# Experts: the prompt's 32 tokens go down in plain float32, a quarter of the output channels in each column quarter of TensorE

## The chip, the cores and the metric
The kernel runs on one core of one Trainium2 chip. The metric is device time in microseconds (us), the median over runs of the whole kernel. TensorE is the matmul engine (PE in the profile, PEld its weight loads), VectorE is DVE, ScalarE is ACT, GpSimd is POOL, and SyncE (SP) issues loads. SBUF is the on-chip memory of 128 partitions, PSUM the memory into which TensorE writes, in banks of 512 float32 per partition.

## The reference, cut to what matters
One layer of a two-branch network over 2048 sample tokens and 256 prompt tokens, 1024 channels wide: a convolution and an attention branch, an output projection, then a mixture of 16 experts in which every expert chooses its tokens, 256 of the samples and 32 of the prompt, and a last norm. All in float32.

```python
def ec_moe(h, w_router, w_g, w_u, w_d):
    B, n, D = h.shape
    cap = EC_FACTOR * n // N_EXPERTS
    aff = jax.nn.softmax((h @ w_router).astype(jnp.float32), axis=-1)
    vals, idx = lax.top_k(aff.transpose(0, 2, 1), cap)
    xg = jax.vmap(lambda hb, ib: hb[ib])(h, idx)
    a = jnp.einsum('becd,edf->becf', xg, w_g)
    u = jnp.einsum('becd,edf->becf', xg, w_u)
    y = jnp.einsum('becf,efd->becd', jax.nn.silu(a) * u, w_d) * vals[..., None].astype(h.dtype)
    return jax.vmap(lambda ib, yb: jnp.zeros((n, D), yb.dtype).at[ib.reshape(-1)].add(yb.reshape(-1, D)))(idx, y)
```

`ec_moe` is called once for the sample tokens (cap 256) and once for the prompt (cap 32), with the same weights; its result is scaled by the gate g2 of the branch and added to x.

## The kernel before, in words
The program is a row of phases, each a block in which every engine has its own instruction list and semaphores order them: front (modulation, first norm, input projection, convolution taps), latents, attention, mix, output projection with the router, ranking (`topk_phase`), experts (`moe_phase`), last norm. Phases don't overlap.

Precision: a product of float32 operands is built from three float32r matmuls. Each operand is split into hi (a rounded copy) and lo (the rest), and hi x hi, hi x lo and lo x hi are added in PSUM. Two places use plain float32 matmuls, which leave two records each in the trace: the values of attention (line 1177), in two column halves of the array, and the rows of the modulation in the front phase (line 388), whose outputs lie at partitions 0, 32, 64 and 96.

`topk_phase` writes `tab` [128, 16 experts, 3, 2]: for each expert three columns of up to 128 tokens (two for the samples, one for the prompt, 32 rows of it used), each with the token's row number and its router value. The prompt's part is ranked first, on 16 partitions, turned by two small transposes (lines 2000 and 2001) and copied into `tab` at the end (lines 1988 and 1989).

`moe_phase` handles an expert in M = 4 pieces of 128 hidden channels; piece q = 4e + m. The first two and the last two experts are written out, the twelve between run in a loop of six turns with two experts each. The engines work as follows, each list in its own order:
- SyncE (lines 2080 to 2090) loads for each piece `raw_gu` (1 MB of gate and up weights) and `raw_d` (512 KB of down weights), two slots of each. A load of `raw_gu` waits until GpSimd has split the piece two back, one of `raw_d` until VectorE has.
- ScalarE makes the hi parts of the weights (lines 2151, 2172), the silu of the gate (2175), the hi part of the hidden vectors (2177) and of the turned tokens (2156).
- GpSimd makes the lo part of gate/up (2112, one instruction of 2048 elements per partition), issues the gathers of an expert's tokens (2098), the scatters of its results (2107, an indirect DMA that adds to rows of x2: 128, 128 and 32 rows of 4 KB), and in the first six pieces the look-ups of later experts' tables (2118).
- VectorE makes the lo part of the down weights (2229), the hidden vectors `hid` = up x silu(gate) (2235), their lo part (2237) and of the tokens (2204), and at m = 0 the scaled result of the expert before: `scale_y` (2212), three instructions of 1024 elements, one per token tile.
- TensorE (lines 2274 to 2310) runs in each piece 48 gate/up matmuls of 288 columns (256 sample tokens and 32 of the prompt), then, for m > 0, four transposes that turn a part of the next expert's tokens, the down matmuls of the piece before for the two sample tiles (12 of 512 columns), four more transposes, and the down matmuls of the third tile (6). In these the hidden vectors are the stationary operand, 128 tokens wide, and the weights of 512 output channels the moving one. The third tile has 32 tokens; `h_hi` and `h_lo` are padded to 128 with zeros. The results of the four pieces add up in `py`, three times two PSUM banks. At m = 1 the first down matmul overwrites `py` and waits for `y_done`, the end of `scale_y`.

In the front phase the rows of the modulation (lines 380 to 389) come behind a tile of the input projection, and ahead of them TensorE waits for its own last matmul:

```python
                    if b == NBL - 1:
                        pe.wait_ge(o_done, n + 1)
                        pe.sem_inc(tile_done, 1)
```

Of the kernel before, what the change touches and what calls it, by code (L numbers as in the profile page):

```python
# [1851 lines left out]
def topk_phase(nc, t, affT, tab, pos, ident):  # L1852
# [13 lines left out]
    with ExitStack() as ctx:  # L1866
# [5 lines left out]
        topp, atp, atpf = p.sb("topp", [E, CAPP]), p.sb("atp", [E, CAPP], U32), p.sb("atpf", [E, CAPP])  # L1872
        cand, low, kept = (p.sb(n, [P, 1], U32) for n in ("cand", "low", "kept"))
# [12 lines left out]
        tp = p.ps("tp", [CAPP, 2, E])  # L1886
# [7 lines left out]
        with nc.Block() as block:  # L1894
# [12 lines left out]
            def _(dve):  # L1907
# [27 lines left out]
                dve.tensor_scalar(atpf[:], atp[:], 1.0, float(S), ALU.mult, ALU.add).then_inc(atp_done, 1)  # L1935
                dve.wait_ge(ld, 16 * LOADS)
# [51 lines left out]
                dve.tensor_copy(tab[0:CAPP, :, 2, 0].bitcast(U32), tp[:, 0]).then_inc(out_done, 1)  # L1988
                dve.tensor_copy(tab[0:CAPP, :, 2, 1], tp[:, 1]).then_inc(out_done, 1)
# [7 lines left out]
            def _(pe):  # L1997
                pe.wait_ge(atp_done, 1)
                pe.wait_ge(max_done, CAPP // 8)
                pe.transpose(tp[:, 0], atpf[:], ident[0:E, 0:E])  # L2000
                pe.transpose(tp[:, 1], topp[:], ident[0:E, 0:E]).then_inc(tp_done, 1)
# [15 lines left out]
def moe_phase(nc, t, tab, pos, ident):  # L2017
# [6 lines left out]

    TOK = CAP + CAPP
    TOKP = 3 * P
    M = FF // P
    SL = ((0, P), (P, P), (CAP, CAPP))
    with ExitStack() as ctx:
        p = Scope(nc, ctx, "moe")  # L2030
        raw_gu, raw_d = p.sb("raw_gu", [P, 2, 2, KD, P]), p.sb("raw_d", [P, 2, D])
# [4 lines left out]
        act_g, hid = p.sb("act_g", [P, TOK]), p.sb("hid", [P, TOK])  # L2036
        h_hi, h_lo = p.sb("h_hi", [P, 2, TOKP], F32R), p.sb("h_lo", [P, 2, TOKP], F32R)
        yo = p.sb("yo", [P, 3, D])
        gate = p.sb("gate", [P, 2, D])
        idx_g, idx_s = p.sb("idx_g", [P, 2, 3], U32), p.sb("idx_s", [P, 2, 3], U32)  # L2040
        val_s = p.sb("val_s", [P, 2, 3])
        bank = [p.ps("g", [P, BLK]), p.ps("u", [P, BLK])]
        py = p.ps("py", [P, 3, D])
        gate_ld = p.sem("gate_ld")
        gu_ld, d_ld = p.sems("gu_ld", 2), p.sems("d_ld", 2)
# [6 lines left out]
        zero_done, may_issue = p.sem("zero_done"), p.sem("may_issue")  # L2052
# [21 lines left out]
        with nc.Block() as block:  # L2074
            @block.sync
            def _(sp):
                for s in range(2):
                    sp.dma_start(gate[:, s], t["mod"][s, 5 * D:6 * D].partition_broadcast(P)).then_inc(gate_ld, 16)

                def load(e, u, first, last):  # L2080
                    for m in range(M):
                        q = M * e + m
                        if not (first and m < 2):
                            sp.wait_ge(glo_done, q - 1)
                        sp.dma_start(raw_gu[:, m % 2], t["w_gate_up"][bass.ds(q, 1)].rearrange("o p g k n -> (o p) g k n")
                                     ).then_inc(gu_ld[m % 2], 16)
# [6 lines left out]
            def _(pool):  # L2093
# [7 lines left out]
                def scatter(e, u):  # L2101
# [4 lines left out]
                    for i, (_, n) in enumerate(SL):  # L2106
                        pool.indirect_dma_start(t["x2"], bass.IndirectOffsetOnAxis(ap=idx_s[0:n, u, i:i + 1], axis=0),
                                                yo[0:n, i], None, compute_op=ALU.add).then_inc(y_st[i], 16)
# [16 lines left out]
                for b in (h_hi, h_lo):  # L2125
                    pool.memset(b[:, :, TOK:].bitcast(F32), 0.0).then_inc(zero_done, 1)
# [20 lines left out]
            def _(act):  # L2147
# [16 lines left out]
                def expert(e, u, first, last):  # L2164
                    for m in range(M):
# [3 lines left out]
                        act.wait_ge(d_ld[slot], 16 * (2 * e + m // 2) + 16)  # L2169
                        if not (first and m < 2):  # L2170
                            act.wait_ge(d_mm, q - 1)
                        act.activation(d_hi[:, slot], raw_d[:, slot], ACT.Copy).then_inc(dhi_done, 1)  # L2172
# [4 lines left out]
                        act.activation(h_hi[:, slot, 0:TOK], hid[:], ACT.Copy).then_inc(hhi_done, 1)  # L2177
# [6 lines left out]
            def _(dve):  # L2184
# [7 lines left out]
                def pick_s(e, u):  # L2192
                    dve.wait_ge(gate_ld, 32)
# [13 lines left out]
                def scale_y(e, u):  # L2207
                    dve.wait_ge(d_mm, M * e + M)
                    dve.wait_ge(pick_s_done, 2 * e + 2)
                    for i, (_, n) in enumerate(SL):  # L2210
                        wait(dve, y_st[i], 16 * e)
                        dve.scalar_tensor_tensor(out=yo[0:n, i], in0=py[0:n, i], scalar=val_s[0:n, u, i:i + 1],
                                                 in1=gate[0:n, i // 2], op0=ALU.mult, op1=ALU.mult).then_inc(y_done, 1)
# [5 lines left out]
                dve.wait_ge(gate_ld, 32)  # L2219

                def expert(e, u, first, last):
                    for m in range(M):
# [6 lines left out]
                        dve.tensor_tensor(d_lo[:, slot], raw_d[:, slot], d_hi[:, slot].bitcast(F32), ALU.subtract  # L2229
# [7 lines left out]
                        dve.tensor_tensor(h_lo[:, slot, 0:TOK], hid[:], h_hi[:, slot, 0:TOK].bitcast(F32), ALU.subtract  # L2237
# [10 lines left out]
            def _(pe):  # L2248
# [7 lines left out]
                def down(q, slot, first_piece, last_piece, part):  # L2256
                    for i in part:
                        for h, w in ((h_hi, d_hi), (h_hi, d_lo), (h_lo, d_hi)):
                            for n in range(2):
                                mm = pe.matmul(py[:, i, n * BLK:(n + 1) * BLK], h[:, slot, i * P:(i + 1) * P],  # L2260
                                               w[:, slot, n * BLK:(n + 1) * BLK],
# [265 lines left out]
```

## Time and profile before

| | us |
|---|---|
| median of 3 runs | 3421.84 |
| lowest, highest | 3418.48, 3424.2 |
| the profiled execution, whole | 3415.4 |
| its span, first to last instruction | 3413.5 |
| TensorE matmuls busy | 3067.7 (90%) |
| VectorE busy | 2008.2 (59%) |
| ScalarE, GpSimd busy | 1031.9, 1008.2 |

The span and all rows below come from the one profiled execution. "Busy" is the union of an engine's instructions. Matmuls overlap in the records, so the duration of one (0.39 us for 512 columns) is longer than the spacing at which they follow each other; costs on TensorE are read from start to start. `128*128 128x512` is a matmul with 128 rows by 128 stationary columns and 512 moving ones.

### The profile page before, as it was taken

What the parts mean: (1) busy time and instruction counts of PE and PEld (TensorE: products, weight loads), DVE (VectorE), ACT (ScalarE), POOL (GpSimd) and SP (SyncE); (2) the same over time, 40 slices, a digit from 0 to 9 for tenths busy, and PEclk for the clock granted to TensorE, in tenths of its full rate; (3) what the DMA queues carried; (4) which work ended last, traced back from release to release, by engine and by line L of the source; (5) the groups of instructions that cost most, each with busy time, mean ns of one, the idle gap of its engine ahead of it and who ended that gap; (6) DMA issues with size and microseconds to landing.
All of it is one profiled execution on the core that took longest, in us unless ns stands there. A gap on an engine that the chain in (4) does not pass through costs nothing. (4 is left out here: it accounts for less than half of the span.)

```text
span 3413.5 us, 44579 instructions
## 1 busy us (share of the span) xinstructions
PE 3067.7 (90%) x17172; PEld 2510.0 (74%) x17172; DVE 2008.2 (59%) x2516; ACT 1031.9 (30%) x1401; POOL 1008.2 (30%) x652
## 2 busy tenths in 40 slices
PE   7999999997969999999999799899925999999990
PEld 7788888885756666666677577778824899999990
DVE  2518384665467777777777645444474555555643
ACT  3411111111433333333333232123302333333332
POOL 0000000000113333333333443211105755655551
PEclk8999999998979999999999999999956999999995
DMA  5312131324320111011010155554304656666656
GB/s 180 112 44 101 65 132 51 108 71 137 144 66 6 29 25 28 14 23 31 6 25 19 52 184 186 191 165 146 124 5 148 186 187 186 203 190 185 187 155 241
DMA packets 135392, 370.16 MB, mean 108 GB/s; under 512 B 19478, under 2 KB 43900, under 8 KB 124828
## 3 DMA queue, kind: packets, MB, share of 16 engines
q1 hardware_dynamic: 97596, 266.60, 23.8%
q0 software_dynamic: 22080, 73.51, 7.6%
q10 hardware_dynamic: 15552, 27.79, 2.2%
q8 instruction: 111, 1.82, 0.2%
q14 instruction: 53, 0.43, 0.0%
HBM read 264.92 MB, written 102.89 MB: 108 GB/s over the span
## 5 line engine op out<-in xcount | busy, mean ns | idle before, releaser
L1231 DVE TENSOR_REDUCE at_mpart<-at_mx 128x2 f32<-128x512 f32 x574 | 369.3, 684 | 168.7 <-PE at_mx L1165 167.4
L1078 ACT ACTIVATE at_w<-at_sc 128x1024 f32<-128x1024 f32 (+1 forms) x296 | 299.4, 1013 | 546.3 <-PE at_sc L1141 515.6
L1119 POOL TENSOR_TENSOR at_part<-at_part,at_w 128x512 f32<-128x512 f32 x224 | 299.7, 1338 | 402.8 <-ACT at_w L1078 399.6
L2112 POOL TENSOR_TENSOR moe_gu_lo<-moe_raw_gu,moe_gu_hi 128x2048 fp32r<-128x2048 f32 x64 | 297.7, 4657 | 134.5 <-ACT moe_gu_hi L2151 134.1
L493 DVE SCALAR_TENSOR_TENSOR fr_r<-fr_r,fr_dw 128x2334 f32<-128x2334 f32 x120 | 318.0, 2650 | 3.9
L368 PE MATMUL fr_po<-hT_hi,fr_w_hi 128*128 128x512 f32 (+1 forms) x800 | 296.9, 371 | 2.1 <-PE fr_tp L368 1.2
L1177 PE MATMUL at_acc<-at_w,V 128*64 128x256 f32 (+1 forms) x2368 | 297.3, 388 | 0.0
L368 PE MATMUL fr_po<-hT_lo,fr_w_hi 128*128 128x512 f32 (+1 forms) x800 | 294.6, 368 | 0.0
L368 PE MATMUL fr_po<-hT_hi,fr_w_lo 128*128 128x512 f32 (+1 forms) x800 | 294.4, 368 | 0.0
L1259 DVE TENSOR_TENSOR at_part<-at_part,at_w 128x512 f32<-128x512 f32 x224 | 262.9, 1174 | 20.0 <-ACT at_w L1078 7.7
L2229 DVE TENSOR_TENSOR moe_d_lo<-moe_raw_d,moe_d_hi 128x1024 fp32r<-128x1024 f32 x64 | 190.2, 2971 | 107.1 <-ACT moe_d_hi L2172 107.1
L1177 PEld LDWEIGHTS at_acc<-at_w,V 128*64 128x64 f32 x2368 | 156.4, 138 | 91.5 <-issue 14.2
L244 POOL DMA_DIRECT2D fr_wm<-w_ada_rows x32 | 16.9, 532 | 649.9 <-PE fr_acc L388 649.9
L368 PEld LDWEIGHTS fr_po<-hT_hi,fr_w_hi 128*128 128x128 f32 x800 | 150.7, 188 | 38.7 <-issue 13.2
L287 ACT ACTIVATE fr_r<-fr_po 128x512 f32<-128x512 f32 (+1 forms) x100 | 55.6, 556 | 390.4 <-PE fr_po L368 390.4
L368 PEld LDWEIGHTS fr_po<-hT_lo,fr_w_hi 128*128 128x128 f32 x800 | 150.7, 188 | 25.4
L368 PEld LDWEIGHTS fr_po<-hT_hi,fr_w_lo 128*128 128x128 f32 x800 | 150.8, 189 | 25.1
L2286 PE MATMUL moe_g<-moe_x_hi,moe_gu_hi 128*128 128x288 f32 x512 | 152.9, 299 | 9.3 <-POOL moe_gu_lo L2112 9.3
L2286 PE MATMUL moe_g<-moe_x_hi,moe_gu_lo 128*128 128x288 f32 x512 | 152.7, 298 | 0.0
L2286 PE MATMUL moe_g<-moe_x_lo,moe_gu_hi 128*128 128x288 f32 x512 | 152.3, 297 | 0.0
L2286 PE MATMUL moe_u<-moe_x_hi,moe_gu_hi 128*128 128x288 f32 x512 | 151.5, 296 | 0.0
L2286 PE MATMUL moe_u<-moe_x_hi,moe_gu_lo 128*128 128x288 f32 x512 | 151.0, 295 | 0.0
(336 smaller groups left out, 7096.7 us busy)
## 6 DMA issues: line engine op xcount, KB each, us to landing
moe_raw_gu<-w_gate_up SPq DMA_DIRECT2D x64, 1024.0 KB, 5.6
moe_raw_d<-w_down SPq DMA_DIRECT2D x64, 512.0 KB, 3.6
fr_wm<-w_ada_rows POOLq DMA_DIRECT2D x32, 512.0 KB, 4.6
gates_scratch<-fr_r ACTq DMA_DIRECT2D x64, 256.0 KB, 2.0
mx_gates<-gates_scratch SPq DMA_DIRECT2D x64, 256.0 KB, 2.9
fr_raw<-w_in SPq DMA_DIRECT2D x28, 512.0 KB, 4.4
fr_r<-x POOLq DMA_DIRECT2D x18, 512.0 KB, 4.5
op_m_raw<-mixed_scratch SPq DMA_DIRECT2D x9, 1024.0 KB, 5.7
```

What stands on the lines that cost most here:

```text
L244: pool.dma_start(wm[:, n % 2].rearrange("p h n -> p (h n)"), t["w_ada_rows"][n]).then_inc(wm_ld[n % 2], 16)
L287: act.activation(stage[:, n % PO, 0:size], po[:, n % PO, 0:size], ACT.Sigmoid if KINDS[j] == "g" else ACT.Copy).then_inc(out_done, 1)
L368: mm = pe.matmul(out[:, 0:size], w[:, s, k, :], h[:, k, tok:tok + size], start=first, stop=final)
L493: dve.scalar_tensor_tensor(out=conv, in0=v[:, w:w + CW], scalar=scalar, in1=conv, op0=ALU.mult, op1=ALU.add).then_inc(taps, 1)
L1078: act.activation(w[:, g % NW, :, 0:n], sc[:, 2 * (g % 2):2 * (g % 2) + 2, 0:n], ACT.Exp, scale=SM_SCALE).then_inc(exp_done, 1)
L1119: pool.tensor_tensor(part[:, j % 2, 1, 0:n], before, w[:, g % NW, 1, 0:n], ALU.add).then_inc(add_p, 1)
L1177: mm = pe.matmul(acc[half * DV:(half + 1) * DV, j % 2, 0:n], V[:, h, key_tiles(b, c) + k, :], w[:, g % NW, k, half * n:(half + 1) * n], st ...
L1231: dve.tensor_reduce(mpart[:, 2 * half:2 * half + 2, c], max_bank(m, half), AX.X, ALU.max).then_inc(red_done[half], 1)
L1259: dve.tensor_tensor(part[:, j % 2, 0, 0:n], before, w[:, g % NW, 0, 0:n], ALU.add).then_inc(add_d, 1)
L2112: pool.tensor_tensor(gu_lo[:, slot], raw_gu[:, slot], gu_hi[:, slot].bitcast(F32), ALU.subtract).then_inc(glo_done, 1)
L2229: dve.tensor_tensor(d_lo[:, slot], raw_d[:, slot], d_hi[:, slot].bitcast(F32), ALU.subtract).then_inc(dlo_done, 1)
L2286: mm = pe.matmul(bank[g][:, 0:TOK], w[:, slot, g, k], x[:, u, k], start=(k == 0 and w is gu_hi and x is x_hi), stop=(k == KD - 1 and x is ...
```

## The change
In the experts' phase the third token tile leaves the common path. Its hidden vectors are taken in plain float32, straight from `hid`, and the down weights straight from `raw_d`; four matmuls of 256 moving columns replace the six of 512. Matmul g computes output channels 256g to 256g + 255 for the 32 tokens and writes them to PSUM partitions 32g to 32g + 31 of `y3` [128, 256]. So the result of the prompt has 128 rows of a quarter of the channels. It is scaled by one VectorE instruction of 256 elements, with the router values repeated four times and a gate laid out in the same way, and scattered as 128 rows of 1 KB with indices 4 x row + g into x2 seen as rows of a quarter. `raw_d` gets four slots, `hid` two, `h_hi` and `h_lo` lose their padding, `tab` a fourth column. The ranking prepares the repeated values and the indices.

```diff
@@ topk_phase
+        quarter, four = p.sb("quarter", [E, 4, CAPP]), p.sb("four", [E, 4, CAPP])
-        tp = p.ps("tp", [CAPP, 2, E])
+        tp = p.ps("tp", [P, 3, E])
                 dve.tensor_scalar(atpf[:], atp[:], 1.0, float(S), ALU.mult, ALU.add).then_inc(atp_done, 1)
+                dve.wait_ge(max_done, CAPP // 8)
+                for g in range(4):
+                    dve.tensor_scalar(quarter[:, g], atp[:], 4.0, float(4 * S + g), ALU.mult, ALU.add).then_inc(atp_done, 1)
+                    dve.tensor_copy(four[:, g], topp[:]).then_inc(atp_done, 1)
-                dve.tensor_copy(tab[0:CAPP, :, 2, 0].bitcast(U32), tp[:, 0]).then_inc(out_done, 1)
-                dve.tensor_copy(tab[0:CAPP, :, 2, 1], tp[:, 1]).then_inc(out_done, 1)
+                dve.tensor_copy(tab[0:CAPP, :, 2, 0].bitcast(U32), tp[0:CAPP, 0]).then_inc(out_done, 1)
+                dve.tensor_copy(tab[:, :, 2, 1], tp[:, 1]).then_inc(out_done, 1)
+                dve.tensor_copy(tab[:, :, 3, 0].bitcast(U32), tp[:, 2]).then_inc(out_done, 1)
-                pe.transpose(tp[:, 0], atpf[:], ident[0:E, 0:E])
-                pe.transpose(tp[:, 1], topp[:], ident[0:E, 0:E]).then_inc(tp_done, 1)
+                pe.transpose(tp[0:CAPP, 0], atpf[:], ident[0:E, 0:E])
+                pe.transpose(tp[:, 1], four[:].rearrange("e g n -> e (g n)"), ident[0:E, 0:E])
+                pe.transpose(tp[:, 2], quarter[:].rearrange("e g n -> e (g n)"), ident[0:E, 0:E]).then_inc(tp_done, 1)
@@ moe_phase, SyncE
-                for s in range(2):
-                    sp.dma_start(gate[:, s], t["mod"][s, 5 * D:6 * D].partition_broadcast(P)).then_inc(gate_ld, 16)
+                sp.dma_start(gate[:], t["mod"][0, 5 * D:6 * D].partition_broadcast(P)).then_inc(gate_ld, 16)
+                for g in range(4):
+                    sp.dma_start(gate3[g * CAPP:(g + 1) * CAPP, :],
+                                 t["mod"][1, 5 * D + g * QD:5 * D + (g + 1) * QD].partition_broadcast(CAPP)).then_inc(gate_ld, 16)
-                        if not (first and m < 2):
-                            sp.wait_ge(dlo_done, q - 1)
-                        sp.dma_start(raw_d[:, m % 2], t["w_down"][bass.ds(q * P, P), :]).then_inc(d_ld[m % 2], 16)
+                        if not first:
+                            sp.wait_ge(d_mm, q - 3)
+                        sp.dma_start(raw_d[:, m], t["w_down"][bass.ds(q * P, P), :]).then_inc(d_ld[m], 16)
@@ GpSimd
+                    pool.indirect_dma_start(t["x2"].rearrange("t (g n) -> (t g) n", g=4),
+                                            bass.IndirectOffsetOnAxis(ap=idx_s[:, u, 3:4], axis=0),
+                                            yo3[:], None, compute_op=ALU.add).then_inc(y_st[2], 16)
-                for b in (h_hi, h_lo):
-                    pool.memset(b[:, :, TOK:].bitcast(F32), 0.0).then_inc(zero_done, 1)
@@ ScalarE
-                        act.activation(h_hi[:, slot, 0:TOK], hid[:], ACT.Copy).then_inc(hhi_done, 1)
+                        act.activation(h_hi[:, slot], hid[:, slot, 0:CAP], ACT.Copy).then_inc(hhi_done, 1)
@@ VectorE
+                    wait(dve, y_st[2], 16 * e)
+                    dve.scalar_tensor_tensor(out=yo3[:], in0=y3[:], scalar=val_s[:, u, 2:3], in1=gate3[:],
+                                             op0=ALU.mult, op1=ALU.mult).then_inc(y_done, 1)
-                        wait(dve, hhi_done, q)
-                        wait(dve, hlo_done, q)
-                        dve.tensor_tensor(hid[:], bank[1][:, 0:TOK], act_g[:], ALU.mult).then_inc(hid_done, 1)
+                        if not (first and m < 2):
+                            dve.wait_ge(hhi_done, q - 1)
+                            dve.wait_ge(hlo_done, q - 1)
+                            dve.wait_ge(d_mm, q - 1)
+                        dve.tensor_tensor(hid[:, slot], bank[1][:, 0:TOK], act_g[:], ALU.mult).then_inc(hid_done, 1)
@@ TensorE
+                def down_prompt(slot, piece):
+
+                    for g in range(4):
+                        mm = pe.matmul(y3[g * CAPP:(g + 1) * CAPP, :], hid[:, slot, CAP:TOK], raw_d[:, piece, g * QD:(g + 1) * QD],
+                                       start=(piece == 0), stop=(piece == M - 1), skip_group_check=True)
+                    mm.then_inc(d_mm, 1)
-                            down(q - 1, 1 - slot, m == 1, m == 0, (0, 1))
+                            down(1 - slot, m == 1, m == 0)
-                            down(q - 1, 1 - slot, m == 1, m == 0, (2,))
+                            down_prompt(1 - slot, (m - 1) % M)
```

## Rows read from the trace of the kernel before

**Rows 1.** Stretches: us, PE, PEld, DVE, ACT, POOL busy (below: PE alone), clock, DMA, GB/s.
```profile
2700.00:3300.00 600.00, 595.95 (x3810) 547.02 (x3809) 340.81 (x314) 228.29 (x291) 347.29 (x132) 1.00 0.61 189
...
2687.20:2690.50 3.30, 3.30 (x15) 0.50 0.68 228
```

**Rows 2.** Timeline, TensorE, a piece without transposes: start, length, what.
```profile
3024.47 0.63 PE L2260 MATMUL moe_py<-moe_d_hi,moe_h_hi 128*128 128x512 f32 x2
...
3028.60 0.29 PE L2286 MATMUL moe_g<-moe_x_hi,moe_gu_hi 128*128 128x288 f32 x1
```

**Rows 3.** Timeline, TensorE: transposes and third tile of a piece with both.
```profile
3004.65 0.60 PE L2253 MATMUL moe_u<-identity,moe_xg 128*128 128x128 f32 x4
3005.00 0.71 PE L2260 MATMUL moe_py<-moe_d_hi,moe_h_hi 128*128 128x512 f32 x2
...
3006.47 0.29 PE L2286 MATMUL moe_g<-moe_x_hi,moe_gu_hi 128*128 128x288 f32 x1
```

**Rows 4.** Timeline around line 388 (four column quarters); then its records in two short windows.
```profile
271.14 0.28 PE L368 MATMUL fr_po<-hT_hi,fr_w_lo 128*128 128x256 f32 x1
271.26 0.28 PE L368 MATMUL fr_po<-hT_lo,fr_w_hi 128*128 128x256 f32 x1
271.68 1.04 PE L388 MATMUL fr_acc<-fr_wm,silu 128*2 128x512 f32 x8
272.65 0.50 PE L368 MATMUL fr_po<-hT_hi,fr_w_hi 128*128 128x512 f32 x1
272.99 0.39 PE L368 MATMUL fr_po<-hT_hi,fr_w_lo 128*128 128x512 f32 x1
...
L388 PE MATMUL fr_acc<-fr_wm,silu x4: 589/591/591, 271.7 to 271.7; 128*2 128x512 f32 x4
...
L388 PE MATMUL fr_acc<-fr_wm,silu x4: 590/592/592, 272.1 to 272.1; 128*2 128x512 f32 x4
```

**Rows 5.** Timeline around line 1177 (two column halves); then first pair and all (ns min/median/max).
```profile
1500.95 0.28 PE L1165 MATMUL at_mx<-room 96*128 96x256 f32 x1
...
1501.16 1.95 PE L1177 MATMUL at_acc<-at_w,V 128*64 128x256 f32 x16
1503.04 0.50 PE L1139 MATMUL at_sc<-room 97*128 97x512 f32 x1
...
L1177 PE MATMUL at_acc<-at_w,V x2: 430/430/430, 1501.2 to 1501.2; 128*64 128x256 f32 x2
...
L1177 PE MATMUL at_acc<-at_w,V x2368: 272/379/690, 995.3 to 1944.9; 128*64 128x256 f32 x192, 128*64 128x128 f32 x6
```

**Rows 6.** Timeline, GpSimd and TensorE, up to the eighth piece.
```profile
2682.30 9.09 POOL L2112 TENSOR_TENSOR moe_gu_lo<-moe_raw_gu,moe_gu_hi 128x2048 fp32r<-128x2048 f32 x2
...
2686.94 0.46 PE L2286 MATMUL moe_g<-moe_x_hi,moe_gu_hi 128*128 128x288 f32 x1 [1.98 <-POOL moe_gu_lo L2112]
```

**Rows 7.** Timeline of an odd expert in the loop: TensorE, GpSimd, VectorE.
```profile
2970.21 0.43 PE L2253 MATMUL moe_u<-identity,moe_xg 32*128 32x32 f32 x4
...
2977.22 9.22 POOL L2112 TENSOR_TENSOR moe_gu_lo<-moe_raw_gu,moe_gu_hi 128x2048 fp32r<-128x2048 f32 x2
...
2979.68 7.08 DVE L2237 TENSOR_TENSOR moe_h_lo<-moe_hid,moe_h_hi 128x288 fp32r<-128x288 f32 x1 [0.51 <-ACT moe_h_hi L2177]
2986.68 3.65 DVE L2212 SCALAR_TENSOR_TENSOR moe_yo<-moe_py,moe_val_s,moe_gate 128x1024 f32<-128x1024 f32 x3
...
2988.97 0.60 PE L2253 MATMUL moe_g<-identity,moe_xg 128*128 128x128 f32 x4
2990.38 0.74 PE L2260 MATMUL moe_py<-moe_d_hi,moe_h_hi 128*128 128x512 f32 x2 [0.81 <-DVE moe_yo L2212]
```

**Rows 8.** Timeline, GpSimd, the second split of an even expert in the loop.
```profile
3027.55 4.63 POOL L2112 TENSOR_TENSOR moe_gu_lo<-moe_raw_gu,moe_gu_hi 128x2048 fp32r<-128x2048 f32 x1 [0.97 <-ACT moe_gu_hi L2151]
```

**Rows 9.** The scatters' issues on GpSimd (ns); VectorE's wait in the ranking.
```profile
L2107 POOL DMA_INDIRECT x_scratch<-moe_yo,moe_idx_s x48: 1335/1556/1903, 2671.8 to 3344.5; - x48
...
2494.87 0.15 DVE L1937 COPY tk_cand<-tk_bits 128x1 uint32<-128x1 uint32 x1 [3.87 <-DMA tk_ones<-rank_ones]
```

More of the change, by code:

```diff
@@ L2035, in moe_phase @@
         x_hi, x_lo = p.sb("x_hi", [P, 2, KD, TOK], F32R), p.sb("x_lo", [P, 2, KD, TOK], F32R)
[L2036 to L2041, printed above, removed]
+        act_g, hid = p.sb("act_g", [P, TOK]), p.sb("hid", [P, 2, TOK])
+        h_hi, h_lo = p.sb("h_hi", [P, 2, CAP], F32R), p.sb("h_lo", [P, 2, CAP], F32R)
+        yo, yo3 = p.sb("yo", [P, 2, D]), p.sb("yo3", [P, QD])
+        gate, gate3 = p.sb("gate", [P, D]), p.sb("gate3", [P, QD])
+        idx_g, idx_s = p.sb("idx_g", [P, 2, 4], U32), p.sb("idx_s", [P, 2, 4], U32)
+        val_s = p.sb("val_s", [P, 2, 4])
         bank = [p.ps("g", [P, BLK]), p.ps("u", [P, BLK])]
-        py = p.ps("py", [P, 3, D])
+        py, y3 = p.ps("py", [P, 2, D]), p.ps("y3", [P, QD])
         gate_ld = p.sem("gate_ld")
-        gu_ld, d_ld = p.sems("gu_ld", 2), p.sems("d_ld", 2)
+        gu_ld, d_ld = p.sems("gu_ld", 2), p.sems("d_ld", M)
         ghi_done, glo_done, dhi_done, dlo_done = (p.sem(n) for n in ("ghi_done", "glo_done", "dhi_done", "dlo_done"))
@@ L2209, in scale_y @@
                     dve.wait_ge(pick_s_done, 2 * e + 2)
-                    for i, (_, n) in enumerate(SL):
+                    for i in range(2):
                         wait(dve, y_st[i], 16 * e)
-                        dve.scalar_tensor_tensor(out=yo[0:n, i], in0=py[0:n, i], scalar=val_s[0:n, u, i:i + 1],
-                                                 in1=gate[0:n, i // 2], op0=ALU.mult, op1=ALU.mult).then_inc(y_done, 1)
+                        dve.scalar_tensor_tensor(out=yo[:, i], in0=py[:, i], scalar=val_s[:, u, i:i + 1], in1=gate[:],
+                                                 op0=ALU.mult, op1=ALU.mult).then_inc(y_done, 1)
+                    wait(dve, y_st[2], 16 * e)
+                    dve.scalar_tensor_tensor(out=yo3[:], in0=y3[:], scalar=val_s[:, u, 2:3], in1=gate3[:],
+                                             op0=ALU.mult, op1=ALU.mult).then_inc(y_done, 1)
                 pick(0, 0)
@@ L2228, in expert @@
                         dve.wait_ge(dhi_done, q + 1)
-                        dve.tensor_tensor(d_lo[:, slot], raw_d[:, slot], d_hi[:, slot].bitcast(F32), ALU.subtract
+                        dve.tensor_tensor(d_lo[:, slot], raw_d[:, m], d_hi[:, slot].bitcast(F32), ALU.subtract
                                           ).then_inc(dlo_done, 1)
@@ L2254, in turn, with down @@
                     mm.then_inc(tp_done, 1)
-                def down(q, slot, first_piece, last_piece, part):
-                    for i in part:
+                def down(slot, first_piece, last_piece):
+                    for i in range(2):
                         for h, w in ((h_hi, d_hi), (h_hi, d_lo), (h_lo, d_hi)):
                             for n in range(2):
-                                mm = pe.matmul(py[:, i, n * BLK:(n + 1) * BLK], h[:, slot, i * P:(i + 1) * P],
-                                               w[:, slot, n * BLK:(n + 1) * BLK],
-                                               start=(first_piece and h is h_hi and w is d_hi),
-                                               stop=(last_piece and h is h_lo))
-                    if part[-1] == 2:
-                        mm.then_inc(d_mm, 1)
-                pe.wait_ge(zero_done, 2)
+                                pe.matmul(py[:, i, n * BLK:(n + 1) * BLK], h[:, slot, i * P:(i + 1) * P],
+                                          w[:, slot, n * BLK:(n + 1) * BLK],
+                                          start=(first_piece and h is h_hi and w is d_hi),
+                                          stop=(last_piece and h is h_lo))
+                def down_prompt(slot, piece):
[3 more added lines that the diff above has]
+                    mm.then_inc(d_mm, 1)
                 for i in range(3):
@@ L2309, in _ @@
                 pe.wait_ge(dlo_done, M * E)
-                down(M * E - 1, 1, False, True, (0, 1, 2))
+                down(1, False, True)
+                down_prompt(1, M - 1)
 def final_phase(nc, t):
```

31 lines of the change are left out of this document (15 added, 16 removed).

## The prediction
> **What bounds the kernel now.** I read the table of stretches first. Between 2700 and 3300 us of the span, which lies wholly inside the expert phase, TensorE is busy 595.95 of 600 us at full granted clock, VectorE 341, GpSimd 347, ScalarE 228, and the DMA share is 0.61 [rows 1]. So this stage is a stream of matmuls without holes, and what TensorE no longer executes there is time won, as long as no other chain takes over. The change touches almost nothing else: it rewrites the last part of each of the 64 pieces (16 experts by 4).
>
> The timeline of TensorE then prices that part. A piece is 48 gate/up matmuls, then the down projection of the piece before: 18 float32r matmuls of 512 columns, six for each of three token tiles, the third being the prompt's 32 tokens padded to 128. In a piece without transposes the 18 start at 3024.47 and the next piece at 3028.60: 4.13 us, so 1.38 us for six [rows 2]. In a piece with transposes the third tile's six run from 3005.00 to 3006.47, 1.47 us [rows 3]; the 0.09 more comes right behind the transposes and I let it stay. **Removed: 1.38 us a piece.**
>
> **What is put in its place.** Four plain float32 matmuls, 128 rows by 32 stationary columns, 256 moving columns each, one in each column quarter. Two places of the trace of before run this kind of work.
> - The front phase computes rows of the modulation with two stationary columns and 512 moving columns, one matmul in each of four column quarters. The group is eight records (each float32 matmul leaves two), starts at 271.68, and the next line starts at 272.65 [rows 4]: 0.97 us. Asked for a short window at 272.0 the trace has four of the records in flight, all begun at 271.7, and at 272.4 the other four, all begun at 272.1 [rows 4]. So four quarters stream side by side, in two rounds. The eight together last 1.04 and one 0.59, so the last begins 0.45 after the first, and less the stagger within four a round is 0.427 for 512 columns. With 256 columns both rounds together should take 0.427 us. What is left of 0.97 - 0.853, 0.115 us, is how long after its stream the next line begins, and that line's second matmul comes at 0.34 instead of the 0.23 us usual for 512 columns (4.13 / 18, rows 2), another 0.105.
> - The attention phase has float32 matmuls of 64 stationary columns in two column halves: 16 records of 256 columns from 1501.16 to 1503.04 [rows 5], 1.88 us. They last 1.95 and one 0.38, so seven rounds of a pair take 1.57, some 0.22 each; one at a time the 16 would take 3.4. The first pair lasts 430 ns against the median 379 [rows 5], so fresh weights cost 0.05 us once. The last matmul ahead began at 1500.95 and its successor would be due 0.12 later (the spacing of 256 columns in rows 4); the group begins at 1501.16, so entering costs 0.09.
>
> The entry in rows 4 is dearer: the last begins at 271.26, a successor is due at 271.38, the group begins at 271.68, 0.30 us late. But there the code waits first for its own last matmul to finish (line 377), which the changed code doesn't do. I take 0.12 for the entry, near rows 5. **Added: 0.427 + 0.12 entry + 0.05 weights + 0.115 + 0.105 behind = 0.82 us a piece**, bounded by 0.74 (0.09, no weights) and 1.05 (entry 0.30, weights of four quarters 0.10). Saved: 0.56 us a piece, between 0.33 and 0.64.
>
> The Trainium skill, in "TensorE: Matmul & The Clock Gate", part 3, measures 2.38 times for three column tiles and 3.07 for four row tiles instead of the ideal. Rows 4 give 8 x 0.427 = 3.4 us of streaming in 0.97, a factor of 3.5. By the page's 3.07 an estimate of the four would be 1.71 / 3.07 = 0.56 us, and the total 8 us less gain. The rows are this kernel's own and decide.
>
> **Where the saving does not arrive.** (1) The first seven pieces. GpSimd there also looks up the tables of the later experts and runs without a break; the last is its splits from 2682.30, and TensorE's gate matmul of the eighth piece waits 1.98 us and begins at 2686.94 [rows 6]. That chain is GpSimd's own, so the six prompt groups executed before it (3.4 us) only lengthen this wait, and 58 groups count. The scatter of the prompt in the place of 32 rows issues 128; 128-row scatters take 1.56 us and the shortest 1.34 [rows 9], so this chain grows by 0.2. The wait is followed by half clock, 2687.2 to 2690.5 [rows 1]; such a stretch doubles the gate matmuls' cost, and a longer wait may add another, up to 1.7 us, which I keep for the range.
> (2) The odd experts inside the loop. GpSimd's two splits run back to back from 2977.22 for 9.22 us, VectorE's short subtraction h_lo begun at 2979.68 lasts 7.08 us beside them, and only then come the three scalings of y, 2986.68 to 2990.33; TensorE, which wants to overwrite those banks, begins at 2990.38 [rows 7]. Its transposes began at 2988.97, and behind four of them the down matmuls otherwise follow 0.35 later [rows 3]; so it loses 1.06 us, in each of the five loop turns that show this wait. This chain starts from the transposes of the piece before last, at 2970.21. From there TensorE will come 2 x 0.56 = 1.12 us sooner. The chain gets 0.8 shorter, because the third scaling handles 256 columns instead of 1024: the three together take 3.65, so 1.25 each, and about 0.45 by proportion with a fixed 0.2. So the waits grow by 0.3 us: 5 x 0.3 = 1.6. In the even experts the second split begins 0.97 us after the first ends [rows 8], the gap through which h_lo slips; it shrinks to 0.4 and stays.
> (3) Tail and the rest. After the last piece the shorter third scaling gives back 0.8 us, once. In the ranking the eight added VectorE operations on 16 partitions (a small copy takes 0.15 [rows 9]) and the widened transpose lie in a wait of 3.87 us for a DMA [rows 9]: nothing; without that cover, 1.2. One more copy at its end: 0.1 us. Three more gate loads are issued on SyncE before the first weights, while TensorE still waits for its first tokens to be gathered: nothing. On SyncE raw_d now has four slots and waits for the down matmuls of four pieces back instead of a VectorE subtraction of two back, which itself follows those matmuls: no later than now, nor is the gate/up load queued behind it. VectorE's new wait for d_mm is met one down projection earlier. The two memsets and their waits lie beside the gather. The scatters land at most a little otherwise: the same bytes in 128 packets of 1 KB for 32 of 4 KB; priced between -1 and +2 us at the tail, taken as 0.
>
> **Sum.** 58 x 0.56 = 32.5; less 1.6, 0.2 and 0.1; plus 0.8: 31.4 us less, say 31. The profiled execution took 3415.4 us for its span of 3413.5, 6.4 less than the median 3421.84; against it the sum is 3384, against the median 3391. The forecast is made on the median: **3391 us**. A measurement of this kernel tells about 0.2%, 6.8 us, from no change.
>
> **Rivals.**
> A. *Each entry drains the array.* The quarters can't begin until the matmuls ahead have left, as with the entry of 0.30 in rows 4, and the quarters' weights take 0.10: 0.427 + 0.30 + 0.10 + 0.22 = 1.05, saved 0.33 a piece. The chain of rows 7 then gets shorter (0.8) by more than TensorE comes sooner (0.66), so 58 x 0.33 + 0.7 + 0.5 = 20, **3402 us**. For it: rows 4. Against: rows 5, where shape and type change too and the entry costs 0.09. The Trainium skill, "TensorEngine Tiling (Array Packing)", key properties, says that changing the tiling mode drains TensorE; by that rule this rival would hold. Chance 0.13.
> B. *Only two quarters at a time.* All full-width evidence is of two halves; rows 4 used two stationary columns, and 32 need the quarters' loads and streams in earnest. Streaming 0.853, with 0.39 around it 1.24, saved 0.14; or, with A's entry, 1.47, lost 0.09. The waits of rows 7 shrink by 0.5 each, or vanish: 58 x 0.14 + 2.6 + 0.5 = 11 less, or 64 x 0.09 more against 5 + 0.5, about nothing. Between them, **3416 us**. Chance 0.06.
> C. *The quarters run one after another* (slower). Place: the same four matmuls of each piece; price 4 x 0.427 = 1.71 + 0.39 = 2.10 against 1.38, +0.72, by 64 pieces 46, less 2 hidden in the wait of rows 6 and 5 from the vanished waits of rows 7: 39 more, **3461 us**. It decides as soon as the four stream for more than 0.99 us, 2.3 times one alone. For it: four different moving operands with full quarters are nowhere in the trace. Against it: rows 4, four different moving operands at once. Chance 0.05.
> D. *GpSimd and VectorE become the bound in every expert.* If h_lo misses its gap [rows 8] or d_lo, blocked beside a split, comes late for gate matmuls, a wait like that of rows 7 meets all 15 experts: ten more by about 1 us, **3401 us**. Chance 0.05.
>
> **How the numbers follow.** Forecast with its own spread 3380 to 3400: 0.71; A 0.13, D 0.05, B 0.06, C 0.05. The range runs from 3378 (0.64 saved a piece and one or two us at the tail, with the medians' spread of 3 us) to 3411 (A with a second stretch of half clock and dearer weights); it leaves out B and C and about 0.07 of the rest. Faster by over 0.2% are the forecast, A and D, less two hundredths for their tails: 0.87; within 0.2% (3415 to 3429) B and A's tail: 0.07; slower mostly C: 0.06.
>
> **What would show it.** Eight records of the new line in each piece, in two groups of four that begin within 0.03 us, 0.21 us apart; from the first of them to the next gate matmul 0.55 us; the next piece's second matmul 0.1 late. Pieces without transposes 0.56 us shorter. The wait before the eighth piece over 5 us. Waits for the scalings in odd experts about 1.35 us. VectorE's third scaling under 0.5 us. If the two rounds begin one by one, C holds; if the spacing from the last matmul ahead exceeds 0.3, A. The forecast is wrong if the expert phase shortens by the right amount per piece and a new wait appears elsewhere, or if anything outside that phase moves by more than 3 us.

## The result and the profile after

| | us | ratio to before, 95% interval |
|---|---|---|
| before, median of 4 | 3423.02 | |
| changed, median of 4 (3379.0 to 3395.21) | 3388.58 | 0.9891 [0.9867, 0.9915] |
| forecast | 3391 | |
| profiled execution, its span | 3382.57, 3380.9 | |

The change takes 34 us off, a full per cent. (The ratios are the record's own and can differ from the quotient of two medians by 0.001; here the medians alone give 0.9899.) All medians, here and below, are of undisturbed executions; the spread look-ups and the two matmuls of 512 columns had one slow execution each, which is left out. The profiled span is 32.6 us shorter than before's. The stretches of TensorE show where, first of the changed kernel and then of the one before, each cut at the first gate matmul, at that of the eighth piece, of the ninth, and of the last; the columns are length, TensorE busy, granted clock, DMA share, GB/s.

```profile
2610.83:2689.28 78.45, 72.86 (x496) 0.97 0.59 187
2689.28:2701.86 12.58, 12.45 (x77) 0.86 0.61 210
2701.86:3293.45 591.59, 584.04 (x4053) 1.00 0.65 196
3293.45:3306.70 13.25, 13.25 (x92) 1.00 0.00 0
```
```profile
2607.90:2686.94 79.04, 76.54 (x485) 0.97 0.58 185
2686.94:2700.18 13.24, 13.24 (x75) 0.87 0.55 199
2700.18:3321.53 621.35, 617.30 (x3944) 1.00 0.61 187
3321.53:3336.00 14.47, 14.47 (x85) 1.00 0.01 1
```

The first seven pieces give 0.6 us, the eighth 0.7, the 55 after it 29.8, the last with the down matmuls behind it 1.2: 32.2 of the 32.6. The phases ahead took 2.9 us more in this execution, and the end of the expert phase gave back 3.2 (below). The 2.9 us lie ahead of the ranking: from the first instruction of the ranking to the first gate matmul both kernels take 123.0 us, so what the change adds to the ranking doesn't show. Over the 13 profiles of this study the first gate matmul begins between 2605.8 and 2621.5 us. So the phases that the change leaves alone scatter by more than most effects below, while the pieces of the expert phase agree to a few hundredths; where the whole times can't decide, the stretches do. TensorE was busy all but 4 us of the long stretch before, now all but 7.6.

A piece without transposes, in the timeline of TensorE, answers to [rows 2]:

```profile
2967.16 0.63 PE L2274 MATMUL moe_py<-moe_d_hi,moe_h_hi 128*128 128x512 f32 x2
...
2969.49 0.63 PE L2274 MATMUL moe_py<-moe_d_hi,moe_h_lo 128*128 128x512 f32 x2
2970.04 0.64 PE L2282 MATMUL moe_y<-moe_raw_d,moe_hid 128*32 128x256 f32 x8
2971.32 0.40 PE L2304 MATMUL moe_g<-moe_x_hi,moe_gu_hi 128*128 128x288 f32 x1 [0.63 <-POOL moe_gu_lo L2122]
```

Twelve matmuls take 2.88 us up to the group, 0.13 more than twelve at 0.229: that is the entry. And one with transposes, with the group's records asked for in two short windows (columns: ns min/median/max, first and last start):

```profile
2982.37 0.64 PE L2282 MATMUL moe_y<-moe_raw_d,moe_hid 128*32 128x256 f32 x8
2982.94 0.40 PE L2304 MATMUL moe_g<-moe_x_hi,moe_gu_hi 128*128 128x288 f32 x1
2983.18 0.30 PE L2304 MATMUL moe_g<-moe_x_hi,moe_gu_lo 128*128 128x288 f32 x1
2983.31 0.29 PE L2304 MATMUL moe_g<-moe_x_lo,moe_gu_hi 128*128 128x288 f32 x1
...
L2282 PEld LDWEIGHTS moe_y<-moe_raw_d,moe_hid x8: 106/108/109, 2982.4 to 2982.4; 128*32 128x32 f32 x8
L2282 PE MATMUL moe_y<-moe_raw_d,moe_hid x4: 403/403/403, 2982.4 to 2982.4; 128*32 128x256 f32 x4
...
L2282 PE MATMUL moe_y<-moe_raw_d,moe_hid x4: 379/379/379, 2982.6 to 2982.6; 128*32 128x256 f32 x4
```

All eight weight loads and the first four matmuls begin together at 2982.4, the other four at 2982.6 (in the records themselves within 0.05 us, and within 0.02), and the gate matmuls go on 0.57 us after the first. The first gate matmul is followed after 0.24 instead of 0.13. So a group costs 0.13 + 0.57 + 0.11 = 0.81 us.

The waits of the odd experts, answering to [rows 7]; VectorE, GpSimd, TensorE:

```profile
2968.56 7.55 DVE L2250 TENSOR_TENSOR moe_h_lo<-moe_hid,moe_h_hi 128x256 fp32r<-128x256 f32 x1 [0.48 <-ACT moe_h_hi L2185]
2976.04 2.46 DVE L2220 SCALAR_TENSOR_TENSOR moe_yo<-moe_py,moe_val_s,moe_gate 128x1024 f32<-128x1024 f32 x2
2978.42 0.47 DVE L2223 SCALAR_TENSOR_TENSOR moe_yo<-moe_y,moe_val_s,moe_gate 128x256 f32<-128x256 f32 x1
...
2966.63 9.19 POOL L2122 TENSOR_TENSOR moe_gu_lo<-moe_raw_gu,moe_gu_hi 128x2048 fp32r<-128x2048 f32 x2
...
2977.81 0.60 PE L2266 MATMUL moe_g<-identity,moe_xg 128*128 128x128 f32 x4
2978.94 0.72 PE L2274 MATMUL moe_py<-moe_d_hi,moe_h_hi 128*128 128x512 f32 x2 [0.54 <-DVE moe_yo L2223]
```

The third scaling takes 0.47 us. The wait for it is 1.13 - 0.35 = 0.78 us, less than before, but there is a second one, which the timeline of the piece without transposes above ends with: the gate matmuls at 2971.32 wait for the first of GpSimd's two splits, 0.70 us more than the group takes (1.27 unrounded, against 0.57). Together 1.48 where before it was 1.06. And before the eighth piece, with one wait already before the sixth (the counterpart of [rows 6]):

```profile
2664.30 0.40 PE L2304 MATMUL moe_g<-moe_x_hi,moe_gu_hi 128*128 128x288 f32 x1 [1.54 <-POOL moe_gu_lo L2122]
...
2689.28 0.40 PE L2304 MATMUL moe_g<-moe_x_hi,moe_gu_hi 128*128 128x288 f32 x1 [3.29 <-POOL moe_gu_lo L2122]
```

4.8 us of waiting in the place of 2.0.

### The profile page after: what moved, and what is told of

Read it like the earlier page. It is cut to its first block and busy times, and to the rows that moved or that the text cites. A ratio compares the mean times of both kernels' runs of the same rounds, so it can differ in the third digit from the quotient of the medians.

```text
span 3380.9 us, 44892 instructions
## 1 busy us (share of the span) xinstructions
PE 3032.8 (90%) x17301; PEld 2452.0 (73%) x17301; DVE 2016.5 (60%) x2525; ACT 1029.9 (30%) x1401; POOL 1018.2 (30%) x650
## 5 line engine op out<-in xcount | busy, mean ns | idle before, releaser
L2304 PE MATMUL moe_g<-moe_x_hi,moe_gu_hi 128*128 128x288 f32 x512 | 159.2, 311 | 17.4 <-POOL moe_gu_lo L2122 15.2
```

The costliest lines, as they stand in the source:

```text
L2304: mm = pe.matmul(bank[g][:, 0:TOK], w[:, slot, g, k], x[:, u, k], start=(k == 0 and w is gu_hi and x is x_hi), stop=(k == KD - 1 and x is ...
```

## The experiments

All ratios are to the kernel before. Unless told otherwise the base is the changed kernel.

**One column quarter.** Is it the concurrency of the quarters, or plain float32 as such?
```diff
-p.ps("y3", [P, QD])
+p.ps("y3", [CAPP, D])
-mm = pe.matmul(y3[g * CAPP:(g + 1) * CAPP, :], hid[...], raw_d[:, piece, g * QD:(g + 1) * QD], ...)
+mm = pe.matmul(y3[:, g * QD:(g + 1) * QD], hid[...], raw_d[:, piece, g * QD:(g + 1) * QD], ...)
```


> The changed kernel, but the four plain float32 matmuls of 256 columns all write partitions 0 to 31 of a y3 of 32 x 1024, so they use one column quarter; with it come back the third scaling of 1024 elements and the scatter of 32 rows of 4 KB. Theory (the gain is that four quarters stream at once): the group streams 1.71 us instead of 0.43, so 1.28 us a piece more than the changed kernel, 64 pieces 82 us, less 5 hidden in GpSimd's chain of the first pieces and 7 from the waits of the odd experts, plus 0.8 for the third scaling: about +70, 3459 us, slower than before by 36. Rival (the gain is plain float32 itself, with its fewer instructions and smaller h parts, and the quarters matter little): within 10 us of 3389. On the tail: if the 2.5 us between the last scatter's issue and the next phase, which the changed kernel saves, come from rows of 1 KB, they are lost again here; if not, they stay saved.

Measured: 3458.81 us, 1.0099 [1.0073, 1.0126], 70 more than the changed kernel, as expected. (It starts two sums in each bank, and part of the prompt's sum is missing from its output; the next run, which starts one in each, has all of it. All matmuls are executed in both.) Its group:

```profile
2972.06 1.91 PE L2280 MATMUL moe_y<-moe_raw_d,moe_hid 128*32 128x256 f32 x8
2973.91 0.40 PE L2302 MATMUL moe_g<-moe_x_hi,moe_gu_hi 128*128 128x288 f32 x1
```

1.85 us instead of 0.57, 1.28 more, to the hundredth the price of rival C. All pieces last 12.1 us or, without transposes, 11.2, and none shows a wait. Some 4 of the 70 us are the third scaling and the end of the phase, which come back with this edit; the rest is the group. So concurrency is the whole gain, and without it the change would have lost 1%.

**The same with two matmuls of 512 columns.** Do the weight loads of the one quarter cost anything?
```diff
-for g in range(4):
-    mm = pe.matmul(y3[:, g * QD:(g + 1) * QD], hid[...], raw_d[:, piece, g * QD:(g + 1) * QD], ...)
+for n in range(2):
+    mm = pe.matmul(y3[:, n * BLK:(n + 1) * BLK], hid[...], raw_d[:, piece, n * BLK:(n + 1) * BLK], ...)
```


> Plain float32 for the prompt in one column quarter, as two matmuls of 512 columns instead of four of 256. The stream is the same, 2 x 0.853 = 1.71 us a piece; with one load of weights per 512 columns instead of per 256. Theory (the stream decides): the pieces last 12.1 us as with four of 256, the whole 3459 us, slower than before by 1%. Rival (the weight loads were a good part of that): each load saved gives 0.1 us, twice two a piece, 20 us less.

Measured: 3452.64 us, the median of three, 1.0105 [1.0069, 1.014]; 3459 was expected, and the three lie between 3450.75 and 3461.26.

```profile
2962.69 1.90 PE L2280 MATMUL moe_y<-moe_raw_d,moe_hid 128*32 128x512 f32 x4
2964.52 0.40 PE L2302 MATMUL moe_g<-moe_x_hi,moe_gu_hi 128*128 128x288 f32 x1
```

1.83 us: half the weight loads save 0.02. The stream is the price; the rival's 20 us don't come.

**The group twice.** Which part of 0.81 us is streaming?
```diff
+                    for again in range(2):
-                    for g in range(4):
+                        for g in range(4):
```


> The group of four quarter matmuls is issued twice in a row in each piece, both added up, so the prompt's result is doubled. Theory (a group is 0.43 us of streaming plus about 0.35 us for entering and leaving, paid once): 0.43 us more a piece, 28 us, less 3 in the first pieces and up to 4 in the odd experts' waits: +21, 3410 us; spacing from the first record to the next gate matmul 1.00 instead of 0.57. Rival (every group costs its whole 0.78 us, weights and all): +44, 3433 us, spacing 1.3. Rival (the stage is by now paced by GpSimd and VectorE): +10 or less.

Measured: 3409.06 us, 0.9948 [0.993, 0.9966], 20 to 23 more than the changed kernel, as the first theory had it. (The prompt's result is doubled.)

```profile
2965.18 1.07 PE L2283 MATMUL moe_y<-moe_raw_d,moe_hid 128*32 128x256 f32 x16
2966.18 0.40 PE L2305 MATMUL moe_g<-moe_x_hi,moe_gu_hi 128*128 128x288 f32 x1
```

1.00 instead of 0.57: the second group costs its 0.43 us of streaming, a quarter of 1.71, and nothing more for its weights. (The records show four rounds, begun 0.24, 0.22 and 0.22 us apart.) The other 0.38 of a group are entering and leaving.

**Three groups of four left out.** Does further saving arrive?
```diff
                 def down_prompt(slot, piece):
+                    if piece != 0:
+                        return
```
(and the down matmuls of the samples raise d_mm in these pieces; each remaining group is a sum of its own)


> Three of the four prompt groups of each expert are left out (only the first 128 hidden channels of the prompt go down), 48 groups less. Theory (TensorE paces except for the chain in the odd experts that starts at the transposes of the piece before last): 48 x 0.78 = 37 us less, of which 4 don't arrive in the first pieces and 2 x 0.78 in each of five or six odd experts only lengthen the waits, 9: -24, 3365 us; the two waits in the odd experts grow from together 1.5 to 3.0 us. Rival (all of it arrives): -37, 3352 us. Rival (GpSimd and VectorE pace the stage): -10 or less.

Measured: 3368.43 us, 0.9844 [0.982, 0.9868]: 18 to 20 less, not 24. The list of TensorE's waits between 2700 and 3270 us (total, times, longest) says where the rest is:

```profile
PE moe_g L2307 <- DVE moe_x_lo L2212: 7.6, 11, 0.7
PE moe_g L2307 <- POOL moe_gu_lo L2122: 6.0, 5, 1.2
PE moe_py L2274 <- DVE moe_yo L2223: 2.6, 5, 0.5
```

The last two are the odd experts'. The one for GpSimd grew, the one for the scaling didn't: from gate to gate the two cost 1.36 and 0.82 us a turn (10.64 us for 9.28, 11.61 for 10.79), 2.2 where 3.0 was expected. So the shortfall isn't theirs. The first line is it, a wait in every expert that was not expected: at the end of m = 3 the transposes are followed by ScalarE's copy, VectorE's subtraction and only then the next gate matmul. The prompt group had covered that chain. In the changed kernel it covers all but 0.2 us (below); with the group doubled it covers the chain again.

**The look-ups spread.**
```diff
-                        if isinstance(e, int) and M * e + m < 6:
-                            for ahead in range(2):
-                                look_up(4 + 2 * (M * e + m) + ahead)
+                        if isinstance(e, int) and M * e + m < 2 * M:
+                            q = M * e + m
+                            for ahead in range(2 if q < 4 else 1):
+                                look_up((4 + 2 * q if q < 4 else 8 + q) + ahead)
```


> Only the look-ups of the later experts' tables are moved: pieces 0 to 3 do two experts each as now, pieces 4 to 7 one each, instead of two in pieces 4 and 5. Theory (the first seven pieces are paced by GpSimd's own chain, so what TensorE saves there doesn't arrive): the wait of 3.4 us before the eighth piece goes, and with it the stretch of half clock behind it (1.6 us): -5, 3384 us; the gate of the eighth piece begins 5 us earlier after the first one. Rival (that wait is a load's or ScalarE's): no change.

Measured: 3381.05 us, the median of three, 0.9876 [0.9842, 0.991], 5 to 8 less than the changed kernel. The times alone, 3375 to 3387 against 3379 to 3395, don't separate the two; its stretches do (first to eighth gate, eighth to ninth, on to the last):

```profile
2612.94:2687.88 74.94, 72.67 (x496) 0.97 0.61 195
2687.88:2698.91 11.03, 10.91 (x80) 1.00 0.73 239
2698.91:3291.71 592.80, 584.35 (x4052) 1.00 0.65 196
```

3.5 us come back ahead of the eighth piece, and 1.5 in it, now at full clock. 1.2 are lost behind, where the waits of an odd expert appear once more.

**The split ahead of the gathers, and both moves (this one and the spread look-ups), on the changed kernel and on the one before; and the changed kernel again, unedited.**
```diff
-                        if m == 0 and not last:
-                            pool.wait_ge(tp_done, 6 * e + 6)
-                            gather(e + 1, 1 - u)
                         if not (last and m == M - 1):
                             split_gu(M * e + m + 1, (m + 1) % 2)
+                        if m == 0 and not last:
+                            pool.wait_ge(tp_done, 6 * e + 6)
+                            gather(e + 1, 1 - u)
```


> The changed kernel; at m = 0 GpSimd first splits the gate/up weights of the next piece and then issues the three gathers, instead of the other way round. Theory (in the odd experts of the loop two waits, for the first split 0.7 us and for the scaled y 0.8 us, come from the gathers that are issued ahead of two splits back to back): the first split ends 4 us sooner, the gathers make the gap in which VectorE's h_lo slips through, both waits go: 1.5 us in each of five or six loop turns, -7 to -9 us against the changed kernel. Rival (the gathers land too late for the transposes of the next piece, 4.7 us later than now): a new wait of 1 to 3 us in each expert, +10 us or more.

> The split ahead of the gathers and the look-ups spread over eight pieces together. If the two act in different places they add up: -7 to -9 and -5, together -13 us against the changed kernel, ratio about 0.986 of before.

> The kernel before with the same two moves. It has one wait of 1.06 us in five odd experts and one of 2.2 us with 1.6 us of half clock before the eighth piece: -5 and -4, together -9 us, ratio 0.997. Then the change by itself, with both sides free of these waits, is worth 64 x 0.6 + 4 at the tail = 42 us against 'both'; if the quarter groups had a hidden cost elsewhere, less.

> The changed kernel once more, on the same chip as the three that follow, as their base: ratio 0.989 to 0.990 of before.

All on one chip:

| | us | ratio, 95% interval |
|---|---|---|
| before | 3421.97 | |
| changed, again | 3386.42 | 0.9893 [0.9873, 0.9912] |
| split first | 3381.22 | 0.9872 [0.9852, 0.9892] |
| both moves | 3374.28 | 0.9852 [0.9831, 0.9874] |
| both moves on before | 3412.47 | 0.9968 [0.9954, 0.9982] |

With the split first the long stretch of 55 pieces takes 583.89 us instead of 591.59, 7.7 less, as expected, and the only wait of TensorE that its list still names there is this:

```profile
PE moe_g L2304 <- issue: 0.3, 2, 0.2
```

The first eight pieces get 1.0 us longer, so 5 to 7 remain. Both moves together give 12 us, where 13 were expected, and on the kernel before 9.5, where 9 were. Between the two kernels that have both, the medians differ by 38.2 us, against 34 to 36 in the plain kernels and 42 expected; 4 and 12 runs that scatter over 10 and 16 us can't tell it from either. The profiles can: from the first gate matmul to that of the last piece the two differ by 32.7 us, the plain ones by 31.0. Short of the expectation are two things. On the changed side the eighth piece still waits (1.8 us, none on the other side) and then runs partly at half clock (12.54 us instead of 11.0), and at the end of each expert 0.2 us is left of the transposes' chain, as the timeline with the split first shows (0.76 from the group to the gate instead of 0.57):

```profile
2964.19 0.64 PE L2282 MATMUL moe_y<-moe_raw_d,moe_hid 128*32 128x256 f32 x8
2964.95 0.40 PE L2304 MATMUL moe_g<-moe_x_hi,moe_gu_hi 128*128 128x288 f32 x1
```

**One look-up less ahead of the eighth piece.** The base is the kernel with both moves.
```diff
-                            for ahead in range(2 if q < 4 else 1):
-                                look_up((4 + 2 * q if q < 4 else 8 + q) + ahead)
+                            for ahead in range((2, 2, 2, 2, 1, 0, 1, 2)[q]):
+                                look_up(4 + (0, 2, 4, 6, 8, 9, 9, 10)[q] + ahead)
```


> The changed kernel with the split ahead of the gathers, and the look-ups of twelve experts dealt to the first eight pieces as 2, 2, 2, 2, 1, 0, 1, 2 instead of 2, 2, 2, 2, 1, 1, 1, 1. In the version before this one a wait of 1.6 us for GpSimd's split and 1.5 us of half clock stood before and behind the eighth piece's gate. Theory (that chain is GpSimd's own instructions in order): one expert's look-up less ahead of it, 2.5 us, takes the wait away and the half clock with it: -3 against that version, ratio about 0.984 of before. Rival (the wait is for ScalarE or a load): no change.

Measured: 3371.09 us, 0.9863 [0.9836, 0.989]; 0.984 was expected, and neither medians nor ratios can tell this version from the last. The eighth piece takes 11.02 us, at full clock, and starts 0.7 us sooner after the first, 2.2 us together. The wait before it shrinks from 1.80 us to 0.42, but one of 2.08 us stands before the third piece, so part of the waiting has only moved. The half clock is not tied to the wait alone: in the profile with the scatters in another order (next), TensorE waits 2.00 us before the eighth piece, as long as in the kernel before, and the granted clock behind it is 1.00. So the 1.5 us of half clock may come or stay away from one execution to the next. Of the kernels that do all the work, these two are the fastest of the study.

**The order of the scatters**, on the kernel before: where do 3 us at the end of the phase come from?
```diff
-                    for i, (_, n) in enumerate(SL):
+                    for i, n in ((2, CAPP), (0, P), (1, P)):
```


> The kernel before, with the prompt's scatter of 32 rows issued ahead of the two of 128 rows. In the kernel before, the last packet of the last scatter has landed 9.8 us before the next phase begins; in the changed one 6.6 us. Theory (it is the last scatter's 32 rows that make the end of GpSimd's list longer): from the last scatter's issue to the next phase 12.8 us instead of 15.2. Rival (it is the presence of any 32-row scatter, or the size of the phase's code): 15 us or more as before.

Measured, in one execution alone: 16.6 us from the last scatter's issue (3342.14) to the next phase's first load (3358.76). The theory that the last scatter's size decides falls. The rival, that any scatter of 32 rows or the size of the phase's code does it, fits, but its two halves were not told apart, and the cause stays open.

## Why the prediction was right, point by point

- **Removed, 1.38 us a piece; added, 0.82; saved, 0.56.** Pieces without transposes went from 10.51 to 9.95 us, 0.56. With transposes, from 11.41 to 10.81, 0.60. The terms: entry forecast 0.12, measured 0.13; from the group's start to the next line 0.59 (0.427 + 0.05 + 0.115), measured 0.57; behind it 0.105, measured 0.11. The weights, 0.05 in the sum, took 0.02: the first round lasts 0.24 us and the others 0.22, with one quarter or four. The choice that mattered was to take the entry from [rows 5] and not from [rows 4], where the code itself waits first. That the code's own wait explains all of the difference between 0.13 and 0.30 was not tested.
- **58 groups count.** The first seven pieces gave 0.6 us though six groups in them were 3.4 us shorter: GpSimd's chain held them, as said, and spreading its look-ups brought 5 us back. The wait before the eighth piece was to exceed 5 us; it was 3.3, with 1.5 before the sixth piece, which I had not placed. The half clock behind it did not double (0.86 and 0.87 of full speed in the two kernels). Nor does it double a gate matmul's cost, as I wrote of [rows 1]: the 15 there follow each other at 0.24 us instead of 0.13, 1.6 us together.
- **The odd experts' waits** grew from 1.06 to 1.48 us, forecast 1.35. The sum was right and the place half wrong: the scaling became a smaller wait (0.78), and the first split, whose slack I had not worked out, a new one (0.70). My 2 x 0.56 = 1.12 us was also too small. From the transposes where the chain begins to the gate matmul that needs the first split, TensorE took 12.37 us before and would now take 11.07, 1.30 less, as the group behind those transposes saves more (0.76 us to the gate for 1.50). The split was through 11.6 us after them, 0.75 ahead, and is through 11.7 after them now. That the sum of the two waits still came near 1.35 is in part luck.
- **The tail.** The third scaling gave 0.8 as forecast: 0.47 us for 1.25. (The fixed 0.2 in its working had no row behind it.) The scatters, bounded by -1 and +2 and taken as 0, were outside: from the last issue to the next phase 12.75 us instead of 15.2, and over the profiles of the study 12.3 to 13.1 in the eight kernels that scatter 128 rows, 15.2 to 16.6 in the five with 32.
- **The range.** Its lower end, 3378, is some 3 us below what its own terms give (0.64 saved a piece, 2 at the tail, 3 for the medians: about 3381). Nothing outside the expert phase was to move by more than 3 us. The phases ahead moved by 2.9 between the two profiles, but they move as much between two profiles of one kernel (3.1 in the two of the changed one), so that sign could tell nothing.
- **Rivals.** C had the right price and did not come. B falls with the four equal starts. A falls with its price: the entry costs 0.13 us, not 0.30. The Trainium skill, "TensorEngine Tiling (Array Packing)", key properties, says that a change of the tiling mode drains TensorE, and gives no price; the traces show no more than these 0.13 us at the entry, and whether they are a short drain no run here tells. The Trainium skill, "TensorE: Matmul & The Clock Gate", part 3, measures a factor of 3.07 for four row tiles; carried over to four column quarters, which the page doesn't do, that is an estimate of 0.56 us of streaming. The doubled group shows 0.43. The whole group goes from 1.85 to 0.57, a factor of 3.2, and that is near the 3.07. D did not come as stated, but it is near: the changed kernel has a new wait of 0.2 us at the end of every expert, for the transposes' chain over ScalarE and VectorE, some 3 us in all, which the sum didn't have; and the run with three groups left out shows that below the present length this chain and GpSimd's take over.

The forecast was 31.4 us less; the measured medians say 34.4, and in the two profiles the expert phase with its end is 35.5 shorter. Of what lies between, the scatters' end accounts for about 2.5, and it was taken as 0. So the mechanism and the price of a piece were right, and the tail and the place of the second wait were not.

## What to carry to other kernels

A narrow product that is padded to the array's width can cost less in plain float32 than as three float32r products, if its columns are dealt to the column quarters (here 0.81 us a piece against 1.38, and 2.09 in one quarter); the trace of the same kernel can show beforehand whether they run at once, by the number of records that start together and the time to the next line. Take the cost of entering such a group from a place where the code has no wait of its own. Where one engine gets faster by a known amount, list the slack of everything it waits for within the same stretch, not only of the wait that shows today: each one with less slack than the saving turns into a new wait. And compare stretches of the changed phase and not only whole times, when the phases beside it scatter by more than the effect.

## What the runs showed of the hardware that was not expected

- Four column quarters with 32 columns each and four different moving operands stream in 0.43 us (the added group of the doubled run), a quarter of the 1.71 us in one quarter (four records of 512 columns, begun 0.43 us apart, in the run with two matmuls of 512). Eight weight loads of 0.11 us start within the first round, and that round is 0.02 us longer than the others.
- The end of the expert phase, from the last scatter's issue to the next phase, is about 3 us shorter in the eight kernels in which the prompt's result is scattered as 128 rows of 1 KB than in the five with 32 rows of 4 KB (medians 12.8 and 15.5). The data are not it: before, the DMA share is nil from 3351 us on, 8.7 us ahead of the next phase; after, from 3321, 6.2 ahead. The stretches of the kernel before and of the changed one (length, GpSimd busy, clock, DMA share, GB/s):

```profile
3348.00:3351.00 3.00, 0.00 (x0) 0.50 0.48 92
3351.00:3354.00 3.00, 0.00 (x0) 0.50 0.00 0
```
```profile
3318.00:3321.00 3.00, 0.00 (x0) 0.50 0.54 94
3321.00:3324.00 3.00, 0.00 (x0) 0.50 0.00 0
```

The longer end comes back with 32 rows in the kernel with one column quarter (15.9 us from the last issue). What fills these microseconds was not found.
